# Renumbering the tokens of a two-layer encoder by grid column, and splitting the first attention's projections in two

## The reference, cut to what matters

```python
def neighborhood_attention(x, w_in, rel_bias, w_out):
    qkv = (x @ w_in).reshape(B, rows, GRID_W, 3, NA_HEADS, NA_HEAD_DIM)
    c0 = np.clip(cols - NA_KW // 2, 0, GRID_W - NA_KW)      # NA_KW = 16, GRID_W = 64
    col_idx = c0[:, None] + np.arange(NA_KW)[None, :]
    ...
        s = jnp.einsum('bqhd,bkqjhd->bhqkj', q_row, k_win) + bias[None]
        p = softmax(s over the kh * NA_KW seen positions)
        return jnp.einsum('bhqkj,bkqjhd->bqhd', p, v_win)
    return o @ w_out

def peer_ffn(x, w_q, sub_keys, u, v):
    ...                                   # top 16 of 256 sums of two top-16 lists
    hid = gelu(einsum('td,ted->te', xt, u[et]))
    return einsum('te,ted->td', gt * hid, v[et])
...
    h = layer_norm(DN_ALPHA * h + mix, ln_mix_g[layer], ln_mix_b[layer])
    ffn = peer_ffn(h, ...)
    h = layer_norm(DN_ALPHA * h + ffn, ln_ffn_g[layer], ln_ffn_b[layer])
```

## Time and profile before

| | us |
|---|---|
| median of 3 runs (1646.4 to 1649.34) | 1648.97 |
| the profiled execution | 1651.84 |
| its span in the trace | 1650.0 |
| first attention, tile 0: first matmul to the end of the last output product | 7.9 to 134.4 |
| norm, head 0's queries and key scores | 134.4 to 148.4 |
| choice of the first experts, first gather issued | 148.4 to 156.3 |
| expert stage of layer 0 | 156 to about 855 |
| end of layer 0, second attention, choice | about 855 to 951 |
| expert stage of layer 1 and last norm | 951 to 1650 |

### The profile page before, as it was taken

How to read it: one execution, slowest core, us unless ns; L and a number is a source line. 1 busy time by engine, 2 the same in 40 slices (tenths; PEclk the granted TensorE clock), 3 DMA queues, 4 the chain that set the end, 5 groups by cost and what they waited for, 6 DMA issues and landing times.

```text
span 1650.0 us, 15957 instructions
## 1 busy us (share of the span) xinstructions
PE 1421.6 (86%) x4970; PEld 748.4 (45%) x4970; DVE 1028.7 (62%) x2800; ACT 483.3 (29%) x1249; POOL 482.7 (29%) x522
## 2 busy tenths in 40 slices
PE   8997889889888889897789979999898888887876
PEld 6776344443354444443245654454334443333332
DVE  1114777767867776576542467666676777776765
ACT  1112334333323333122222333333333222222222
POOL 0001233333333333333310023333332333333331
PEclk9998899999999999999998979999999999999999
DMA  9622999999999999999972099999999999999996
GB/s 351 227 85 79 421 402 414 421 401 420 421 419 417 421 421 418 421 399 405 421 298 77 29 366 405 404 399 418 391 421 419 409 393 422 421 422 421 420 414 274
DMA packets 92692, 602.64 MB, mean 365 GB/s; under 512 B 10432, under 2 KB 10688, under 8 KB 26432
## 3 DMA queue, kind: packets, MB, share of 16 engines
q0 software_dynamic: 73728, 536.90, 79.1%
q1 hardware_dynamic: 18880, 64.72, 10.2%
HBM read 600.53 MB, written 1.05 MB: 365 GB/s over the span
## 4 chain that ended last, share of the span: by engine, by line
PE 39%; DMA 32%; DVE 21%; issue 4%; ACT 3%; DVEq 2%; POOL 0%; SPq 0%; POOLq 0%; ACTq 0%
DMA uv<-in_peer_uv_dram,expert 31%; PE y L478 20%; DVE uv L1244 10%; PE px L272 4%; PE spare L378 3%; PE y L344 3%; PE y L281 2%; ACT diag L938 1%; PE spare L295 1%; DVE key_idx L1151 1%; DVE key_left L1143 1%; PE spare L309 1%; PE spare L308 1%; DVE key_idx L1145 1%; DVE pos L1168 1%
## 5 line engine op out<-in xcount | busy, mean ns | idle before, releaser
L478 PE MATMUL y<-uv,diag 128*128 128x512 f32 x2048 | 974.5, 617 | 176.7 <-ACT diag L938 175.7
L1244 DVE CUSTOM_DVE_ANT_0 uv<-px,uv 128x1024 f32<-128x1024 f32 x512 | 618.7, 1220 | 349.6 <-DMA uv<-in_peer_uv_dram,expert 347.8
L828 POOL DMA_INDIRECT uv<-in_peer_uv_dram,expert x512 | 481.5, 940 | 1144.0 <-PE y L478 864.4
L478 PEld LDWEIGHTS y<-uv,diag 128*128 128x128 f32 x2048 | 378.2, 195 | 668.2 <-issue 380.1
L938 ACT ACTIVATE diag<-ident,wts 128x128 f32<-128x128 f32 x512 | 177.9, 394 | 456.5 <-DVE wts L1250 439.2
L932 ACT ACTIVATE act_hid<-hid 128x2 f32<-128x2 f32 x260 | 52.8, 203 | 484.3 <-DVE hid L1244 481.1
L1063 DVE TENSOR_TENSOR probs<-spare,bias 128x512 f32<-128x512 f32 x16 | 11.0, 689 | 97.5 <-PE spare L295 97.5
L272 PE MATMUL px<-hT,uv 128*128 128x256 f32 x256 | 59.3, 392 | 7.9 <-DMA uv<-in_na_w_dram 7.9
L932 ACT ACT_TABLE_LOAD x48 | 61.6, 1283 | 0.8
L272 PEld LDWEIGHTS px<-hT,uv 128*128 128x128 f32 x256 | 50.2, 197 | 17.4 <-issue 10.4
L1250 DVE TENSOR_TENSOR wts<-act_hid,gate 128x2 f32<-128x2 f32 x260 | 40.6, 156 | 15.9 <-ACT act_hid L932 15.9
(11 more groups left out here) (189 smaller groups left out, 1135.5 us busy)
## 6 DMA issues: line engine op xcount, KB each, us to landing
uv<-in_na_w_dram SPq DMA_DIRECT2D x24, 512.0 KB, 9.1
uv<-in_peer_uv_dram,expert POOLq DMA_INDIRECT x512
wb_rows<-in_peer_w_q_dram SPq DMA_DIRECT2D x16, 512.0 KB
bias<-in_na_bias_dram SPq DMA_DIRECT2D x16, 256.0 KB, 3.1
uv<-in_na_w_out_dram SPq DMA_DIRECT2D x8, 512.0 KB, 5.4
wb_rows<-in_na_w_out_dram SPq DMA_DIRECT2D x8, 512.0 KB
uv<-in_mla_w_out_dram SPq DMA_DIRECT2D x8, 512.0 KB, 10.8
wb_rows<-in_mla_w_out_dram SPq DMA_DIRECT2D x8, 512.0 KB
```

The lines of the kernel that those rows point to most:

```text
L478: last = T.matmul(Y[t][:, c, :], diag[:, n % RING, :], uv[:, n % RING, 1, c * 512:(c + 1) * 512], start=False, stop=(k == TOPK - 1 and g % ...
L828: pool.indirect_dma_start(uv[:, n % RING, :, :].rearrange("p h d -> p (h d)"), None, uv_table, bass.IndirectOffsetOnAxis(ap=expert[:, g, k ...
L1244: V_.tensor_tensor_reduce(out=rows, in0=px[:, :, :], in1=rows, scale=1.0, scalar=0.0, op0=ALU.mult, op1=ALU.add, accum_out=hid[:, k:k + 1] ...
```

## The change

Tokens are numbered column by column. Tile 0 is then columns 0 to 31, and the farthest key that its queries see is in column 39, so token 159; tile 1's queries see tokens 96 to 255. Each tile's scores, bias and softmax cover 160 keys (`SPAN`), not 256; the rest of the 256-wide probabilities is set to zero once, and transposes and weighted values stay as they were.

The first attention projects keys for 160 tokens and queries for 128. The other 96 keys (`rest_of_keys`) and 128 queries (`rest_of_queries`) come from the same weights later: pair 0 while DVE does the norm, pair 1's keys behind the norm's transposes, its queries and pairs 2 to 5 and the keys of 6 during the choice, the queries of 6 and both of 7 in expert steps 1, 6 and 7. For that the K and Q items 0 to 6 (without Q6) each keep a piece of `uv`, and Q6, K7 and Q7 lie in `wb_rows`; V and O items pass through six pieces that are the memory of kept heads 3 to 5, whose query weights are loaded once the attention has ended. POOL's gather into slot n waits until the rest of pair n is projected. Head 1's queries move behind the rests, head 2's into expert steps 2 and 3 with key scores in 5; the seeds of tile 1 into steps 5 and 8; DVE's first choice within the expert stage from steps 0, 2, 4, 6 to 4, 6, 8, 10.

```diff
+THROUGH = 6
+SPAN = 160
+REST = TOK - SPAN
+SEEN = [(0, SPAN), (REST, TOK)]
...
-        bias = sb("bias", [P, BIAS_RING, 2, TOK])
+        bias = sb("bias", [P, BIAS_RING, 2, SPAN])
...
+        through = [kept[h][c] for h in range(3, KEPT) for c in range(2)]
...
+        aside = [("Q", 6), ("K", 7), ("Q", 7)]
...
+        def rest_bank(j):
+            return 6 if j == PAIRS - 1 else 2 + j % 2
...
-            def project(part, j, b, w, some):
-                for k in some:
-                    last = T.matmul(B[b][:, 0:TOK], w[:, k, :], hT[:, k, :], start=(k == 0), stop=(k == DK - 1))
+            def project(part, j, b, w, width):
+                for k in range(DK):
+                    last = T.matmul(B[b][:, 0:width], w[:, k, :], hT[:, k, 0:width], start=(k == 0), stop=(k == DK - 1))
...
+            def rest_of_keys(j):
+                b = rest_bank(j)
+                w = item("K", j)
+                bank_free(b)
+                for k in range(DK):
+                    last = T.matmul(B[b][:, 0:REST], w[:, k, :], hT[:, k, SPAN:TOK], start=(k == 0), stop=(k == DK - 1))
+                if j == 6:
+                    last.then_inc(s_k6, 1)
+
+            def rest_of_queries(j):
+                b = rest_bank(j)
+                w = item("Q", j)
+                for k in range(DK):
+                    last = T.matmul(B[b][:, P:2 * P], w[:, k, :], hT[:, k, P:TOK], start=(k == 0), stop=(k == DK - 1))
+                last.then_inc(s_full[b], 1)
+                filled(b, ("rest", j))
...
-                last = T.matmul(B[6][:, i * TOK:(i + 1) * TOK], QQ[i * HD:(i + 1) * HD, t, j, :],
-                                Kt[i * HD:(i + 1) * HD, j, :], start=True, stop=True)
+                last = T.matmul(B[6][:, i * SPAN:(i + 1) * SPAN], QQ[i * HD:(i + 1) * HD, t, j, :],
+                                Kt[i * HD:(i + 1) * HD, j, slice(*SEEN[t])], start=True, stop=True)
...
+                    if layer == 0 and at in (2, 3):
+                        queries(0, 2, at - 2, 7)
+                    if layer == 0 and at == 5:
+                        key_scores(0, 2, 7, 7)
...
+                if layer == 0:
+                    if at == 1:
+                        rest_of_queries(6)
+                    if at == 6:
+                        rest_of_keys(7)
+                    if at == 7:
+                        rest_of_queries(7)
+                    if at in (5, 8):
...
+                        seed(1, (at - 5) // 3)
...
+                if layer == 0:
+                    rest_of_keys(0)
+                    rest_of_queries(0)
                 norm_transposes(mix0, 0, 6)
                 norm_transposes(mix0, 1, 7)
+                if layer == 0:
+                    rest_of_keys(1)
                 hT_ready(mix0, (6, 7))
...
                 key_scores(layer, 0, 6, 7)
+                if layer == 0:
+                    rest_of_queries(1)
+                    for j in range(2, 5):
+                        rest_of_keys(j)
+                        rest_of_queries(j)
                 seed(0, 1)
                 load_px(layer, 0)
+                if layer == 0:
+                    rest_of_keys(5)
+                    rest_of_queries(5)
+                    rest_of_keys(6)
+                    queries(0, 1, 0, 6)
+                    queries(0, 1, 1, 6)
+                    key_scores(0, 1, 6, 7)
+                    return
...
             out_product(PAIRS - 1, ...)
-            for b in (2, 3):
-                bank_free(b)
-            for half in range(2):
-                seed(1, half)
...
+                    if before in aside:
+                        sp.wait_ge(s_full[rest_bank(before[1])], job["rest", before[1]])
...
-                if 2 <= j:
-                    kept_load(0, j - 2)
-            line_load("O", PAIRS - 1, na_w_out[PAIRS - 1])
+                if 3 <= j < 6:
+                    kept_load(0, j - 3)
+            through_load("O", PAIRS - 1, na_w_out[PAIRS - 1])
+            sp.wait_ge(s_full[3], job["V", PAIRS - 1])
+            sp.wait_ge(s_y, PAIRS)
+            for h in range(3, KEPT):
+                kept_load(0, h)
...
-                    sp.dma_start(out[0, t * P:(t + 1) * P, c * 512:(c + 1) * 512], xh[:, c * 512:(c + 1) * 512])\
+                    by_column = out[0, :, c * 512:(c + 1) * 512].rearrange("(r w) d -> w r d", r=ROWS)
+                    sp.dma_start(by_column[t * P // ROWS:(t + 1) * P // ROWS, :, :], xh[:, c * 512:(c + 1) * 512])\
...
                         if n >= RING:
                             pool.wait_ge(s_acc, n - RING + 1)
+                        elif n < 6:
+                            pool.wait_ge(s_full[rest_bank(n)], job["rest", n])
+                        elif n == 6:
+                            pool.wait_ge(s_k6, 1)
...
+            def store_rest(j):
+                b = rest_bank(j)
+                act.wait_ge(s_full[b], job["rest", j])
+                A.activation(Kt[:, j, SPAN:TOK], B[b][:, 0:REST], ACT.Copy)
+                A.activation(QQ[:, 1, j, :], B[b][:, P:2 * P], ACT.Copy, scale=NA_SCALE).then_inc(s_free[b], 1)
...
+                    store_rest(1)
+                    store_rest(2)
+                    gate_exp(layer, 0)
+                    for j in range(3, 6):
+                        store_rest(j)
...
-                first = 2 if g == PH - 1 else 0
+                first = 4 if (layer, g) == (0, 0) else 2 if g == PH - 1 else 0
```

More of the change, by code:

```diff
@@ L165, in program @@
         s_line = [sem(f"line_item_landed{i}") for i in range(LINE)]
+        s_through = [sem(f"value_or_out_rows_landed{i}") for i in range(THROUGH)]
+        s_k6 = sem("rest_of_keys6_projected")
         s_wb = [sem(f"side_item_landed{i}") for i in range(WB)]
@@ L257, in line_item, with through_item, item @@
                 return line[:, n % LINE, :]
+            def through_item(part, j):
+                n = through_no[part, j]
+                pe.wait_ge(s_through[n % THROUGH], 16 * (n // THROUGH + 1))
+                return through[n % THROUGH]
+            def item(part, j):
+                w = side_item(part, j) if (part, j) in aside else line_item(part, j)
+                return w.rearrange("p (k n) -> p k n", k=DK)
             def side_item(*name):
@@ L289, in scores_na @@
                 if i == 0:
-                    pe.wait_ge(s_free[4], job["K", j])
-                    pe.wait_ge(s_free[5], job["Q", j])
+                    if t == 0:
+                        pe.wait_ge(s_free[4], job["K", j])
+                        pe.wait_ge(s_free[5], job["Q", j])
+                    else:
+                        pe.wait_ge(s_free[rest_bank(j)], job["rest", j])
                     bank_free(6)
@@ L598, in scores_and_values @@
                 project_v(j, w, steps[1:])
-            project("K", 0, 4, item("K", 0), range(DK))
-            project("Q", 0, 5, item("Q", 0), range(DK))
+            width = {"K": SPAN, "Q": P}
+            project("K", 0, 4, item("K", 0), width["K"])
+            project("Q", 0, 5, item("Q", 0), width["Q"])
             for half in range(2):
@@ L609, in _ @@
                         bank_free(b)
-                        project(part, j + 1, b, w, range(DK))
+                        project(part, j + 1, b, w, width[part])
                 transposes(j)
@@ L684, in _, with through_load @@
         def _(sp):
-            na_banks = {"K": 4, "V": 3, "Q": 5}
             def line_load(part, j, src):
                 n = line_no[part, j]
-                if LINE <= n < 4 * PAIRS:
-                    before = [name for name, no in line_no.items() if no == n - LINE][0]
+                if part == "O":
+                    slot = (n % LINE) // 2
+                    sp.wait_ge(s_acc, STEPS - RING + slot + 1)
+                sp.dma_start(line[:, n % LINE, :], src).then_inc(s_line[n % LINE], 16)
+            def through_load(part, j, src):
+                n = through_no[part, j]
+                if n >= THROUGH:
+                    before = [name for name, no in through_no.items() if no == n - THROUGH][0]
                     if before[0] == "O":
@@ L693, in line_load @@
                     else:
[L694 to L698 removed]
+                        sp.wait_ge(s_full[3], job[before])
+                sp.dma_start(through[n % THROUGH], src).then_inc(s_through[n % THROUGH], 16)
             def side_load(src, *name):
@@ L724, in na_load @@
             def na_load(j):
-                for s, part in enumerate("KQV"):
-                    line_load(part, j, na_w[j, s])
+                for part, s in (("K", 0), ("Q", 1)):
+                    if (part, j) in aside:
+                        side_load(na_w[j, s], part, j)
+                    else:
+                        line_load(part, j, na_w[j, s])
+                through_load("V", j, na_w[j, 2])
             for half in range(2):
@@ L956, in side @@
                         store_oT(n)
+                if layer == 0:
+                    if a == 1:
+                        store_rest(6)
```

(12 more changed lines are left out.)

81 lines of the change are left out of this document (46 added, 35 removed).

## The result

| | before, us | changed, us | ratio, 95% interval |
|---|---|---|---|
| first comparison | 1649.15 | 1635.42 (1633.4 to 1637.26) | 0.9919, 0.9901 to 0.9937 |
| `again`, the same kernel once more | 1647.45 | 1631.86 (1630.74 to 1637.4) | 0.9902, 0.9883 to 0.9921 |

Faster by 13.7 us and 15.6 us, where 25.2 was forecast; 1635.42 lies 0.4 us above the range. The changed kernel's profiled execution took 1633.40 us, span 1631.6.

A forecast was written before the change was run, and what follows sets the result against it. TensorE bounds the first attention, gather bytes the expert stage. -26.1 attention, -2.6 norm and clock, +1.8 early steps, +2.6 bytes, -0.9 hole give -25.2: 1626.6 from the profiled run, 1623.8 as median; range 1616 to 1635.

The forecast's parts named there:

- Attention: First attention: narrower projections and scores save 26.1 us of TensorE time, bounds 23.6 and 26.5.
- Norm and clock: Norm to head 0's queries: rests fill PE's idle time, the clock stays up; 2.98 gained, 0.4 lost, 2.6 us net.
- The gathers' new wait: After T0 (end of head 0's key scores): gather 5 leaves at T0 + 17.8, waiting for rests; nothing lost.
- The early steps: Expert steps 1 to 8: 11.1 us more PE work leaves 1.8 us of dry transfers, bounds 0 and 11.1.
- The lag at gather 19: Early expert steps: PE reaches T0 + 61.3 against gather 19 at T0 + 55.3 before, 6.0 us behind.
- The stock: Transfers outstanding at gather 19, plus side item O8, absorb 4.2 us of PE's lag.
- The catch-up: Expert stage: by add 23 PE is at T0 + 89.2, where gather 31 stood before, so the lag is gone.
- Bytes: Expert stage: net 1.08 MB more costs 2.6 us; a hole PE left that later bytes fill gives back 0.9.
- B: Expert stage: none of PE's added work is absorbed, 11.1 us lost instead of 1.8; 1633 us, chance 0.17.
- A: Expert stage gives nothing back: holes elsewhere absorb bytes and lag, none of 3.5 us paid; 1620.3 us, chance 0.15.
- C: Clock falls in the norm anyway and stays low in the rests, holding up gather 5; 1642 us, chance 0.07.
- D: Attention: 160 columns cost as 256 do, losing 10.1 us of projections and 2.5 of scores; 1636.4 us, chance 0.03.

The follow-up runs named there:

- rests_behind_scores: Changed kernel with rests of pair 0 and pair 1's keys moved from the norm to behind head 0's key scores; 1643.38 us, ratio 0.9964.
- gate_beside_exps: Changed kernel plus early gelu table, head 2's queries behind head 1's key scores, first gate's exponential at ACT step 2, late rests' copies one step later; 1625.03 us.
- small_o_items: Changed kernel with the three side items in the expert stage loaded with 128 of 1024 columns, output not the reference's; 1635.03 us, ratio 0.9911.
- choice_at_0: Changed kernel with DVE's first choice back at expert steps 0, 2, 4, 6 and the gate's exponential at ACT's step 1; 1638.87 us, ratio 0.9943.
- pe_kept_warm: Changed kernel with 24 more 128-column PE instructions, results unread, in the hole ahead of the first add; 1629.74 us, ratio 0.9906.
- light_late_rests: Changed kernel, early gelu table, head 2's queries behind head 1's key scores, rests in steps 1, 6, 7 cut to 2 of 8 slices (wrong output); 1623.07 us.
- head2_before_stage: Changed kernel with head 2's queries and key scores back ahead of the expert stage, behind head 1's; 1629.24 us, ratio 0.9887.
- rests_before_stage: Changed kernel with the rests of pair 6's queries and pair 7 moved ahead of head 1's queries, out of steps 1, 6, 7; 1634.39 us, ratio 0.992.
- gelu_table_early: Changed kernel with ACT's gelu table loaded behind the rests' copies instead of behind head 1's key scores; 1629.49 us, ratio 0.9887.

## Why the prediction was wrong, and where it was right

**Attention (26.1 forecast): 27.0.** The last output product ends at 105.41 + 1.96 = 107.37, was 134.41. Keys and queries of a pair 3.96 (forecast 3.97), pair 0 6.73 (6.7), the scores 0.35 less a pair instead of 0.31; the 0.08 wait in front of the scores is gone too. Pricing 160 columns on the line between 128 and 256 held, and no load was waited for. (The farthest column that tile 0's queries see is 38, token 155, not 39; the width of 160 comes from tile 1, tokens 96 to 255.)

**Norm and clock (2.6): 2.7.** 96 columns cost 1.76 / 16 = 0.110 each, just what 128 do: the nearest row was right. The Trainium skill ("TensorE: Matmul & The Clock Gate", "LDWEIGHTS (loading the stationary operand)") has a weight load cost by its own columns; this trace agrees. The clock stayed at 1.00, and `rests_behind_scores` shows 6.39 us in the other case.

**The gathers' new wait (0): nearly 0.** Gather 5 left at 136.77 = T0 + 18.1 (forecast 17.8), and the transfers' share from 130 to 140 was 0.97, which is 0.4 us short of full.

**The early steps (1.8): this step failed.** The forecast had the first add done at T0 + 26.2, gather 19 at T0 + 61.3, and caught up at gather 31, T0 + 89.2. The trace has 31.4, 71.1 and 104.3. The steps of the sum, in their order:
- *The lag at gather 19, forecast 6.0, was 15.8.* PE's list was summed as if PE waited for nothing. ACT's order stood in the text only as a rival. The holes were 2.24, 2.49 and 1.57 us, and the half clock took 1.8 more in the first trace and 6.3 in `again`. In the first trace that is 8.1 of the 9.8 us that were missing; the other 1.7 is spread over PE's list, as work and short waits. With the handoffs repaired and the same PE work, gather 16 moves from -13.9 and -10.5 to -22.0, the lag at gather 19 to 7.5, and the time from 13.7 and 15.6 us under before to 23.3, within 2 us of the forecast, which is in part luck, for the lag was larger than forecast and the catch-up smaller.
- *The stock, forecast 4.2 us of lag for free, is neither shown nor refuted.* Take a share of 1.01 as full and add up what 14 stretches of 10 us miss, from 160 on before and from 130 on in the others: 0.9 us before, 10.3 in the changed kernel, 3.7 in `gate_beside_exps`. The lags at gather 16 are 15.8 and 7.8, the transfers missed beyond before's 9.4 and 2.8. By this measure some 5 to 6 us of lag were not paid. By gather 255 the lags are 13.7 and 3.7, and by that measure it was 2 and 4. No run tests the stock alone, so its size stays open.
- *The catch-up, forecast 6.0 us between gathers 19 and 31, was 0.7,* and 2.0 in `gate_beside_exps`. Its sum of 27.9 us of PE work was too small. The two tables of those stretches, before and then `gate_beside_exps`:

```profile
203.63:237.56 33.93, 29.71 (x106) 14.89 (x104) 25.81 (x74) 13.20 (x32) 11.26 (x12) 1.00 1.01 418
181.60:213.49 31.89, 29.38 (x106) 14.89 (x104) 24.02 (x71) 13.04 (x31) 11.24 (x12) 1.00 0.99 399
```

Before, PE was busy 29.71 of 33.93 us there at full clock, so at most 4.2 could be won back. Of its two waits, 1.64 us in front of transposes and 2.59 in front of a diagonal, 0.41 and 2.10 are still there in `gate_beside_exps`. The second, a wait for a chain through DVE and ACT, came along with the work.

**Bytes (2.6, less 0.9): not seen.** In the changed kernel 1.38 MB less moved none of gathers 8 to 24. In `gate_beside_exps` the question stays open.

**The rivals.** B comes nearest, and part of its reason is right: ACT waited for head 2's queries and key scores of PE's later steps, which made the hole of 2.49. It named neither the gelu table nor the rest of pair 7, nor the half clock in the expert stage. That its 1633 lies within 2.4 us of both medians is in part luck: it takes all 11.1 us of added PE work as lost, where some of the lag was absorbed and the holes, which it did not price, took more. The range took it in with no room above. A, C, D and E did not occur; the clock stayed up where C feared for it and fell elsewhere.

**Not settled:** why the shift wanders where the code is the same. A part can be seen. From layer 0's last gather to layer 1's first, before and most kernels take 110.3 to 110.5 us (two 108.9, `small_o_items` 112.1), with PE at half clock for 10 to 14 us of the second attention; `choice_at_0`, whose clock stays at 1.00 there, takes 104.1; with less half clock than most, `pe_kept_warm` takes 105.8 and `light_late_rests` 107.1. Tables of stretches, changed kernel and `choice_at_0`:

```profile
865.00:875.00 10.00, 10.00 (x31) 5.13 (x30) 3.18 (x10) 3.29 (x11) 0.00 (x0) 0.57 0.18 70
865.00:875.00 10.00, 10.00 (x41) 4.83 (x39) 3.92 (x12) 3.81 (x13) 0.00 (x0) 1.00 0.45 161
```

Why it falls in one execution and not in another, with PE busy throughout in both stretches, stays open. So does the wandering within layer 1, up to 3.6 us (`small_o_items`, -12.2 to -15.8), and how much of the shifts belongs to the profile of before, against which all are taken.

## What to carry to other kernels

Work that is moved beside full transfers isn't free just because its engine has idle time there: ask what each idle piece waits for, and if that is a chain through other engines it moves along. List what is queued behind every new wait on the engines that only copy; here three such places, with the half clock behind the first, cost 8 us at gather 16, and moving copies and table loads by a step or two and head 2's queries into the first hole brought all of it back without touching the arithmetic. When a stage starts with an engine waiting, fill that hole first: here it paid for itself and for the clock. A lag isn't a loss until the transfers run dry: compare the tables of stretches, not only the starts of the gathers.

## What the runs showed of the hardware

Ahead of the first add, a hole of 2.24 or 2.25 us in PE's work was followed by half clock in all six traces that have it (both of the changed kernel, `head2_before_stage`, `rests_before_stage`, `small_o_items`, `rests_behind_scores`); a hole of 0.73 us there was not, and the 1.57 in front of step 8's diagonals was not in any of nine. The hole of 2.48 or 2.49 in front of step 6's transposes was followed by half clock in four traces (`again`, `gelu_table_early`, `rests_before_stage`, `rests_behind_scores`) and not in four (the changed kernel's first, `small_o_items`, `pe_kept_warm`, `choice_at_0`). So the length of the hole alone doesn't decide it. How long the half clock stayed differed between executions of one kernel: 3.48 us of one add, or over 8 us of work. Streaming 96 columns past a fresh 128-column float32 weight load takes the time of 128 (0.110 us an instruction), 160 take 0.136 ((3.96 - 1.78) / 16).
